# One block in place of nine for the branches of a second model's layer, with the sparse attention's values projected feature-major and turned on TensorE

## The reference

```python
def second_block(x, ...):
    for l in range(DEPTH):
        h = rmsnorm(x, attn_norm_w[l])
        proj = h @ w_in[l]
        (z, xbc, dt_raw, sc_b, sc_c, sc_h, q, k_c, v_c, k_s, v_s, k_w, v_w,
         g_nsa) = jnp.split(proj, split_at, axis=-1)
        y_ssd = ssd_mixer(z, xbc, dt_raw, ...)
        y_sc = sc_b * causal_dwconv(sc_c * sc_h, sc_conv_w[l])
        y_nsa = nsa_mixer(q, k_c, v_c, k_s, v_s, k_w, v_w, g_nsa, ...)
        x = x + jnp.concatenate([y_ssd, y_sc, y_nsa], axis=-1) @ w_out[l]
        h = rmsnorm(x, ffn_norm_w[l])
        ...
```

## Time and profile before

| | us |
|---|---|
| median of 2 runs (4588.11 to 4590.89) | 4589.5 |
| the profiled execution | 4589.26 |
| its span in the profile | 4587.5 |
| layer 0 of the second model, first matmul of its branches to the start of its attention | 2990.1 to 3272.1 |
| the same of layer 1 | 3785.5 to 4067.3 |

### The profile page before, as it was taken

How to read it: one execution, slowest core, us unless ns; L and a number is a source line. 1 busy time by engine, 2 the same in 40 slices (tenths; PEclk the granted TensorE clock), 3 DMA queues, 4 the chain that set the end, 5 groups by cost and what they waited for, 6 DMA issues and landing times. The chain is left out here.

```text
span 4587.5 us, 53132 instructions
## 1 busy us (share of the span) xinstructions
PE 4016.8 (88%) x19582; PEld 3037.8 (66%) x19582; DVE 2268.3 (49%) x3774; ACT 1573.5 (34%) x2671; POOL 299.2 (7%) x292
## 2 busy tenths in 40 slices
PE   4896988998999898878899899886879988678998
PEld 2553566777788795645666688664568877456886
DVE  7777674223653562355532555243455524454552
ACT  2044534112442442245421343233344423333431
POOL 1201010001000000000000100102010010201001
PEclk8997999999999999989999999997899999788999
DMA  6602020111222352000022233220123322012332
GB/s 234 202 8 69 18 96 29 56 61 53 92 96 99 115 165 85 35 17 10 24 69 87 81 98 99 81 75 19 38 64 97 100 98 79 14 33 73 96 98 81
DMA packets 83413, 348.84 MB, mean 76 GB/s; under 512 B 9152, under 2 KB 9536, under 8 KB 79680
## 3 DMA queue, kind: packets, MB, share of 16 engines
q1 hardware_dynamic: 69440, 296.59, 20.0%
q0 software_dynamic: 13824, 50.34, 3.4%
HBM read 344.80 MB, written 2.10 MB: 76 GB/s over the span
## 5 line engine op out<-in xcount | busy, mean ns | idle before, releaser
L556 DVE TENSOR_TENSOR split_low<-weight_ring,split_high 128x1024 fp32r<-128x1024 f32 (+1 forms) x412 | 534.3, 1297 | 818.5 <-ACT split_high L548 818.2
L548 ACT ACTIVATE split_high<-weight_ring 128x1024 fp32r<-128x1024 f32 (+1 forms) x430 | 477.9, 1113 | 969.5 <-PE banks L1197 466.2
L1325 PE MATMUL banks<-normed_high,split_high 128*128 128x512 f32 (+1 forms) x1760 | 652.5, 371 | 79.1 <-DVE normed_low L440 37.9
L1325 PE MATMUL banks<-normed_low,split_high 128*128 128x512 f32 (+1 forms) x1760 | 650.1, 369 | 0.0
L1325 PE MATMUL banks<-normed_high,split_low 128*128 128x512 f32 (+1 forms) x1760 | 649.7, 369 | 0.0
L1325 PEld LDWEIGHTS banks<-normed_high,split_high 128*128 128x128 f32 x1760 | 333.9, 190 | 139.9 <-issue 84.4
L1325 PEld LDWEIGHTS banks<-normed_low,split_high 128*128 128x128 f32 x1760 | 334.1, 190 | 55.4
L1325 PEld LDWEIGHTS banks<-normed_high,split_low 128*128 128x128 f32 x1760 | 333.7, 190 | 55.1
L1197 PE MATMUL banks<-hidden_high,split_high 128*128 128x512 f32 (+1 forms) x880 | 325.0, 369 | 7.2 <-DVE split_low L556 7.2
L1197 PE MATMUL banks<-hidden_low,split_high 128*128 128x512 f32 (+1 forms) x880 | 324.5, 369 | 0.0
L1197 PE MATMUL banks<-hidden_high,split_low 128*128 128x512 f32 (+1 forms) x880 | 324.4, 369 | 0.0
(11 more groups left out here) (235 smaller groups left out, 6550.7 us busy)
## 6 DMA issues: line engine op xcount, KB each, us to landing
weight_ring<-in_up SPq DMA_DIRECT2D x220, 512.0 KB, 3.5
weight_ring<-in_down SPq DMA_DIRECT2D x80, 704.0 KB, 4.0
modulation_ring<-in_ada POOLq DMA_DIRECT2D x96, 512.0 KB, 4.5
weight_ring<-in_merge SPq DMA_DIRECT2D x48, 768.0 KB, 4.2
weight_ring<-in_out SPq DMA_DIRECT2D x32, 512.0 KB, 3.5
weight_ring<-in_diff SPq DMA_DIRECT2D x12, 1024.0 KB, 5.5
weight_ring<-in_xbc SPq DMA_DIRECT2D x16, 512.0 KB, 3.7
weight_ring<-in_window SPq DMA_DIRECT2D x6, 1024.0 KB, 4.8
```

What stands on the lines that cost most here:

```text
L548: act.activation(k.splits[0][:, (n0 + panel) % RING, 0:width], k.slot(n0 + panel)[:, 0:width], ACT.Copy).then_inc(k.high_ready.sem, 1)
L556: dve.tensor_tensor(k.splits[1][:, s, 0:width], k.ring[:, s, 0:width], k.splits[0][:, s, 0:width].bitcast(F32), ALU.subtract).then_inc(k.l ...
L1325: last = pe.matmul(sums(r, half), w, x, start=(c + j == 0), stop=(c == KT - 1 and j == 2))
```

## The change

Blocks 1 to 9 become one block (the norm at its start is kept). Every engine has one hand-written order:

- The four narrow jobs for dt and the gates become one full job with features on the partitions (`steps2`, dt in rows 0 to 7 and gates in rows 32 to 43, the rest zeros), first of all; a few transposes turn the result. The four narrow jobs for the values become one full job (job 24), whose tile four transposes turn (`turn_values`), with a copy by ACT. There are 25 full jobs now: 0 steps, 1 to 8 convolved, 9 to 12 z, 13 to 18 short convolution, 19 to 23 keys and queries, 24 values.
- Results rotate through three PSUM banks; the other five serve the branches' own products.
- Between two jobs TensorE takes a piece of the branches' work: the steps' transposes behind job 5, x's behind job 9, C B^T behind jobs 10 and 11, one head around each of jobs 13 to 20 (spread, job, four weighings), the swaps of rope, the compression and the norm's sums behind jobs 21 to 24.
- DVE's and ACT's operations of steps, short convolution, rope, gather, norm and compression stand between the splits of the panels.
- The compression's weights no longer pass through the ring; four DMAs on SP's queue bring 2 MB into tiles that the state space has left.
- The ring of split panels is 1024 wide here instead of 1408, and the branches have 40 tiles instead of 35.

The diff, cut to its core:

```diff
-    with k.nc.Block() as block:
-        normalise(block)
-        project_split(k, [tile_job(m, tile[:, 24 + m, :]) for m in range(6)], 6, lambda panel: KT * P, block)
-    short_convolution(k, [tile[:, 24 + m, :] for m in range(2)], [tile[:, 26 + m, :] for m in range(2)],
-                      [tile[:, 28 + m, :] for m in range(2)],
-                      k.vec(f"sc_conv{l}").rearrange("p (a b) -> p a b", a=3), [mixed[:, 4 + m, :] for m in range(2)])
...
-    jobs += [token_job(12, t, 20, token_major[:, t, :]) for t in range(4)]
-    project_split(k, jobs, 13, lambda panel: KT * (P if panel < 12 else 20))
...
-    step_sizes(k, l, token_major, gates, rows, columns)
-    state_space(k, l, tile[:, 12:16, :], tile[:, 8:10, :], tile[:, 10:12, :], tile[:, 16:20, :],
...
-    jobs += [token_job(5, t, P, values[:, t, :]) for t in range(4)]
-    project_split(k, jobs, 6, lambda panel: KT * P)
...
-    rope(k, [(q[:, 0, :], "64"), (q[:, 1, :], "64"), (both, "64", 64), (ks, "64"), (kw, "64")])
...
-    compress(k, l, both, gathered, hid_rows, hid, cmp_keys, cmp_values)
...
+CONVOLVED = 8
+GATED = range(1 + CONVOLVED, 5 + CONVOLVED)
+HEADS = 8
+WITH_HEADS = 5 + CONVOLVED
+LAST_JOB = WITH_HEADS + 11
...
+    def bank(q):
+        return k.psum[:, q % 3, 0:LAT]
+    def stored(q):
+        return k.product_stored(1 if q == 0 else q + 1 - CONVOLVED)
+    def turned(r):
+        return stored(WITH_HEADS + 6 + r)
...
+        @block.sync
+        def _(sp):
+            for panel in range(LAST_JOB + 1):
+                sp.wait_ge(*k.low_ready(panel + 1))
+                k.load_panel(sp, n0 + panel + RING)
+                if panel == WITH_HEADS + HEADS:
+                    sp.wait_ge(*k.output_ready(4 * HEADS))
+                    for part in range(4):
+                        sp.dma_start(cmp_weights[:, part, :], k.inp[f"cmp2_{l}"][part]).then_inc(
+                            k.blocks_landed.sem, 16)
...
+            def job(q):
+                pe.wait_ge(*k.low_ready(q + 1))
+                if q >= 3:
+                    if 1 <= q - 3 <= CONVOLVED:
+                        pe.wait_ge(*k.taps_added(3 * (q - 3)))
+                    else:
+                        pe.wait_ge(*stored(q - 3))
+                for c in range(KT):
+                    if q == 0:
+                        pe.wait_ge(*k.normed_ready(c + 1 - KT))
+                    for i, (w, u) in enumerate(triple(split_parts(k, n0, q, c * P),
+                                                      (highs[:, c, :], lows[:, c, :]))):
+                        last = pe.matmul(bank(q), w, u, start=(c + i == 0), stop=(c == KT - 1 and i == 2))
+                last.then_inc(k.product_ready.sem, 1)
...
+            def spread_total(h):
+                if h >= 2:
+                    pe.wait_ge(*k.decay_argument(4 * (h - 1)))
+                else:
+                    pe.wait_ge(*k.turned_copied(8))
+                pe.matmul(select_bank(h), k.table("select")[0:8, h * P:(h + 1) * P], total, start=True,
+                          stop=True).then_inc(k.scores_ready.sem, 1)
+            def weigh_head(h):
+                rows = slice(64 * (h % 2), 64 * (h % 2) + 64)
+                if h >= 4 and h % 2 == 0:
+                    pe.wait_ge(*k.output_stored(h - 3))
+                for j in range(4):
+                    n = 4 * h + j
+                    pe.wait_ge(*k.weights_ready(n + 1))
+                    pe.matmul(pair_bank(h // 2)[rows, j * P:LAT], xdt[:, j, 64 * h:64 * h + 64],
+                              k.probs[:, n % 4, j * P:LAT], start=(j == 0), stop=(j == 3)).then_inc(
+                                  k.output_ready.sem, 1)
...
+            def swap(r):
+                pe.wait_ge(*turned(r))
+                if r >= 1:
+                    pe.wait_ge(*k.sine_part(r))
+                pe.matmul(k.psum[:, 7, 0:LAT], k.table("swap_64"), turns[r][0], start=True, stop=True).then_inc(
+                    k.rope_swapped.sem, 1)
...
+            def turn_values():
+                pe.wait_ge(*stored(LAST_JOB))
+                for t in range(4):
+                    last = pe.transpose(k.psum[:, 4, t * P:(t + 1) * P], mixed[:, 7, t * P:(t + 1) * P],
+                                        k.table("ident"))
+                last.then_inc(k.steps_turned.sem, 1)
...
+            job(0)
+            for m in range(CONVOLVED):
+                job(1 + m)
+                if m == 4:
+                    turn_steps()
+            job(9)
+            turn_x()
+            job(10)
+            products_of_group(0)
+            job(11)
+            products_of_group(1)
+            job(12)
+            for h in range(HEADS):
+                spread_total(h)
+                job(WITH_HEADS + h)
+                weigh_head(h)
+            job(21)
+            swap(0)
+            swap(1)
+            job(22)
+            swap(2)
+            multiply_blocks()
+            job(23)
+            swap(3)
+            turn_blocks()
+            sum_squares()
+            job(LAST_JOB)
+            swap(4)
+            pe.wait_ge(*k.block_gated(2))
+            pe.matmul(k.psum[:, 5, 0:B], w2[:, 0:P], hid[:, 0:B], start=True, stop=True)
+            pe.matmul(k.psum[0:B, 3, 0:64], hid[:, 32:32 + B], w2[:, P:P + 64], start=True, stop=True).then_inc(
+                k.block_product.sem, 1)
+            turn_values()
...
+            def next_high(q):
+                if q < LAST_JOB:
+                    split_high(k, act, n0, q + 1, KT * P, k.product_ready(q) if q else None)
...
+            for h in range(HEADS):
+                next_high(WITH_HEADS + h)
+                for j in range(4):
+                    n = 4 * h + j
+                    act.wait_ge(*k.decay_argument(n + 1))
+                    view = k.probs[:, n % 4, j * P:LAT]
+                    act.activation(view, view, ACT.Exp).then_inc(k.decay_ready.sem, 1)
+                store(WITH_HEADS + h, scale=64 ** -0.5 if WITH_HEADS + h == 20 else 1.0)
+            next_high(21)
+            store(21, scale=64 ** -0.5)
+            next_high(22)
+            store(22)
+            next_high(23)
+            act.wait_ge(*k.block_product(1))
+            act.activation(hid_rows, k.psum[0:64, 3, 0:P], ACT.Gelu_apprx_tanh).then_inc(k.block_gated.sem, 1)
+            for c in range(4):
+                act.wait_ge(*k.output_stored(2 * c + 2))
+                act.activation(k.probs[:, c, 0:LAT], mixed[:, c, :], ACT.Square).then_inc(k.squares_ready.sem, 1)
+            store(23)
+            act.wait_ge(*k.block_product(2))
+            act.activation(hid, k.psum[:, 4, 0:64], ACT.Copy).then_inc(k.block_gated.sem, 1)
+            act.wait_ge(*k.squares_summed(1))
+            act.activation(k.probs[:, 0, 0:LAT], k.psum[:, 6, 0:LAT], ACT.Sqrt, bias=k.scalars[:, 12:13],
+                           scale=1.0 / 512).then_inc(k.deviation_ready.sem, 1)
+            store(LAST_JOB)
+            act.wait_ge(*k.block_product(3))
+            act.activation(cmp_keys, k.psum[:, 5, 0:B], ACT.Copy)
+            act.activation(cmp_values, k.psum[0:B, 3, 0:64], ACT.Copy)
+            act.wait_ge(*k.steps_turned(2))
+            act.activation(tile[:, 33, :], k.psum[:, 4, :], ACT.Copy)
...
+            def next_low(q):
+                if q < LAST_JOB:
+                    split_low(k, dve, n0, q + 1, KT * P, k.high_ready(q + 2))
...
+            next_low(1)
+            taps(0)
+            dve.wait_ge(*k.steps_argument(2))
+            dve.tensor_scalar(r1, r2, 1.0, None, ALU.add).then_inc(k.steps_value.sem, 1)
+            dve.wait_ge(*k.steps_value(2))
+            link(dve.tensor_scalar(r3, r1, -1.0, None, ALU.add))
+            link(dve.tensor_scalar(r5, r3, 1e-30, None, ALU.max))
+            link(dve.reciprocal(r5, r5))
+            next_low(2)
+            taps(1)
...
+            for h in range(HEADS):
+                dve.wait_ge(*k.scores_ready(h + 1))
+                for j in range(4):
+                    n = 4 * h + j
+                    if n >= 4:
+                        dve.wait_ge(*k.output_ready(n - 3))
+                    dve.tensor_scalar(k.probs[:, n % 4, j * P:LAT], select_bank(h)[:, j * P:LAT],
+                                      columns[:, 16 * j + 8 + h:16 * j + 9 + h], 0.0, ALU.subtract,
+                                      ALU.min).then_inc(k.decay_argument.sem, 1)
+                next_low(WITH_HEADS + h)
+                if h >= 2 and h % 2 == 0:
+                    finish_pair(h // 2 - 1)
+                if h >= 6:
+                    convolve(h - 6)
+            next_low(21)
+            finish_pair(3)
+            rotate(0)
+            gather()
+            rotate(1)
+            next_low(22)
+            rotate(2)
+            next_low(23)
+            rotate(3)
+            dve.wait_ge(*k.deviation_ready(1))
+            dve.reciprocal(k.probs[:, 1, 0:LAT], k.probs[:, 0, 0:LAT]).then_inc(k.inverse_ready.sem, 1)
+            rotate(4)
+            dve.wait_ge(*k.inverse_ready(1))
```

(11 more changed lines are left out.)

612 lines of the change are left out of this document (267 added, 345 removed).

## The result

The changed kernel takes 4433.3 us, the median of two runs (4430.6 to 4436.1), against 4589.5 before: a ratio of 0.966, with an interval of 0.962 to 0.970. It is faster by 3.4%. The profiled execution is the one of 4430.6 us; its span is 4428.8.

The account below looks back on a forecast made before the run. Seams between blocks were taken to leave TensorE idle 62 of 282.0 us per layer; the terms 138.6 + 6.8 + 7.5 + 28.3 + 17.5 + 4.6 + 6 gave 209.3, so 4589.3 - 145.4 = 4444 us, range 4424 to 4482.

Parts of the forecast that it names:

- some 15: Sign of being right: TensorE idle some 15 us between the branches' first matmul and the attention's first.
- jobs (one at half clock, 24 at 5.44): 25 full jobs per layer: the first 8.0 us at half clock, the other 24 at 5.44, 138.6 us.
- pauses at jobs 3, 4, 5 and 8: Early jobs: TensorE waits for DVE's splits behind step-size work, 3.6, 1.7 and 0.5 us, then DVE catches up.
- 16 transposes, 8 products: State space's small work on TensorE: 7.5 us per layer, bounds 6.5 and 8.4.
- eight heads beside their jobs: State-space heads: 3.54 us of TensorE each, 28.3 for eight; with its job a head takes 9.0 us.
- behind the heads, and the tail: Swaps, compression and sum of squares with a transpose 17.5 us, then the tail with the attention's start 4.6.
- clock: Half-clock loss behind two pauses, step sizes and compression: 3 us each, 6 per layer, bounds 0 and 16.
- costs nothing: ACT's share of the step sizes is hidden, since a job hides 3.4 us of ACT; otherwise 7.0 us.
- the reserve: In each head, POOL's last weight comes 0.4 us early, plus about 2 more since TensorE asks for it last.
- contention: Rival: DVE and POOL hinder each other in the heads, up to 2 us a head, 4476 us; 14 in 100.
- The clock did not stay low: Rival: jobs and small products run at half clock through the heads, 54 us a layer, 4552 us; 5 in 100.
- Anything outside the two stretches that changed by more than 2 us: Sign of being wrong: a change over 2 us outside the rewritten branch stretches of the second model's two layers.

Follow-up runs that it names:

- the last kernel: Changed kernel with splits ahead of the step sizes, scaling before the last key's turn, and next high half always ahead of the Silu: 4415.6 us, ratio 0.9605.
- the spread-behind-the-job kernel: Changed kernel with each head's spread product behind its job instead of ahead of it: 4526.0 us, ratio 0.986.
- the kernels with more POOL work: Changed kernel with two or four useless 128x256 POOL multiplications added per head: 4443.0 us (0.968) with two, 4474.5 us (0.974) with four.
- the scaling-first kernel: Changed kernel with DVE scaling the four normed tiles before turning the last key: 4430.4 us, ratio 0.965.
- the last two: Changed kernel with splits first and scaling first together, 4426.0 us; and the same with the pause left at job 6 also removed, 4415.6 us.
- measured again: The changed kernel, unaltered, run once more as reference beside the first three experiments: 4436.1 us, ratio 0.966.

## Why the prediction was right, point by point

The forecast was 4444 us, the result is 4433.3, inside the range of 4424 to 4482 and faster as expected. Of the 11 us, 9.6 are in the two stretches (155.0 measured for 145.4); in the profiled runs the first model gives 7.7 more and the attentions take 4.1 back. TensorE was idle 10.3 us in the stretch of layer 0, not the "some 15" that were named as a sign.

Laid out along layer 0, each term beside what the trace has:

| term | predicted | measured |
|---|---|---|
| jobs (one at half clock, 24 at 5.44) | 138.6 | 138.6 |
| pauses at jobs 3, 4, 5 and 8 | 3.6 + 1.7 + 0.5 + 0 | 3.64 + 0 + 1.00 + 1.28 |
| turns of the step sizes | 1.0 | 1.25 |
| 16 transposes, 8 products | 7.5 | 6.4 |
| eight heads beside their jobs | 28.3 | 28.5 |
| behind the heads, and the tail | 22.1 | 21.8 |
| clock | 6 | 1.8 |
| sum | 209.3 | 204.3 |

**The jobs.** From 2982.34 to the first pause, which begins at 3001.22, are 18.88 us: 8.0 + 2 x 5.44 to the hundredth. The jobs' own cost held everywhere that no pause was near.

**The pauses.** The first was worked out from DVE's queue at 3.6, and it is 3.64. The second, 1.7 at job 4, did not appear, for a reason that the prediction kept in another term: behind the first pause job 3 ran partly at half clock and took 6.93 us (3004.86 to 3011.79), and meanwhile DVE had job 4's low half ready, at 3011.73. The clock's loss and this pause are the same time, and the sum had them both. The third, predicted 0.5, is 1.00. The fourth, at job 8, was not predicted at all, and it is ACT's. That ACT's share of the step sizes "costs nothing" was a step that failed: it cost 1.28 us a layer. The total, 5.9 us for 5.8, agrees by luck: one pause too many and one too few. The 3.4 us of room in a job held on average, but the gates' Sigmoid and the Silu behind it each need a table load of 1.28 us, and both stand ahead of the high half of that job. ACT's timeline:

```profile
3030.74 0.78 ACT L1724 ACTIVATE branch_tiles<-banks,small_vectors 128x512 f32<-128x512 f32 x1 [4.14 <-PE banks L1576]
...
3031.71 1.28 ACT L1740 ACT_TABLE_LOAD   x1
3033.00 0.21 ACT L1740 ACTIVATE branch_tiles<-banks 128x48 f32<-128x48 f32 x1
3033.23 1.28 ACT L1702 ACT_TABLE_LOAD   x1
...
3035.06 1.05 ACT L557 ACTIVATE split_high<-weight_ring 128x1024 fp32r<-128x1024 f32 x1
```

and DVE's, which waits for it:

```profile
3036.14 1.23 DVE L565 TENSOR_TENSOR split_low<-weight_ring,split_high 128x1024 fp32r<-128x1024 f32 x1 [2.27 <-ACT split_high L557]
```

The centre tap could not start before job 6 ended (3030.6), and from there ACT has 5.4 us of queue in front of a job that is needed 5.4 us later, with DVE's 1.2 still to come. The room of a job must be counted from the wait it starts behind, not as idle time. With the high half ahead of them, as in the last kernel, the loads cost nothing. The Trainium skill (ScalarE: Activation LUTs, What ACT_TABLE_LOAD costs) adds to each load of about 1.28 us another 1.38 for draining; the load's 1.28 agrees, and the drain is not here: the Sigmoid starts 1.29 us after its load does, and 0.02 us lie between the operation ahead of the first load and the load.

**The heads** came at 9.01 us for 9.0. The reasoning that a job hides the head's chain held: the spread-behind-the-job kernel is the counter-proof (15.3 us a head in layer 0, 13.9 in layer 1), and the kernels with more POOL work measure the reserve. The reserve was put at 0.4 for the last weight and about 2 more, without contention; 1.3 are left with the contention's 1.15 in it, so the 2.4 were right and half of them are used.

**Behind the heads** the second swap waits 0.87 (predicted 0.75), the 64 products of the compression take 7.4 us, not 8.3 (they now follow each other without a pause between panels; the 8.3 was four times a panel by itself), the squares 3.1, not 3.6. Nothing waits for the compression's four transfers. The tail is 4.64 us for 4.6, with TensorE idle 3.52 of it ("about 5" was named as a sign); the scaling-first kernel shows that 2.2 of it was DVE's order.

**The clock** was the mis-sized term: 6 taken, 1.8 measured. It makes 8.4 of the 9.6 us. Inside the block only the 3.64 us pause has a price in clock. The two jobs behind it, 48 matmuls, take 12.7 us in place of 10.9 (3004.86 to 3017.57); in TensorE's timeline the first seven of them start 0.42 to 0.59 us apart, the rest mostly 0.23. Behind the pauses of 1.00 and 1.28 us the very next matmuls stand 0.33 and then 0.23 apart, full clock. The prediction charged 3 us each to the step sizes and to the compression, and the compression has no pause long enough: 0.98 granted. One such pause at the 2.5 us of the earlier trace rows would have given 205.8.

**The transposes and products** were taken from a stretch that ran partly at half clock; between jobs they run at the full one, 16 transposes in 1.7 us and eight products in two lots of 2.1, with 0.6 us in the seams with the jobs.

TensorE's timeline around them:

```profile
3048.44 1.91 PE L1593 MATMUL banks<-ones_and_identity,branch_tiles 128*128 128x128 f32 x16
3050.10 0.48 PE L1576 MATMUL banks<-normed_high,split_high 128*128 128x512 f32 x1
...
3055.64 2.32 PE L1602 MATMUL banks<-branch_tiles 128*128 128x512 f32 x8
```

**The other rivals.** The clock did not stay low, and no pause for a bank's store appeared. "Anything outside the two stretches that changed by more than 2 us" was named as a sign against: the attentions with their feed-forwards grew by 2.2 and 1.9. TensorE's busy time there is 1.8 us larger with the same matmuls in layer 0 (471.04 against 469.26), so it is clock: the first row is the kernel before, the second the kernel after, five microseconds from the start of the attention, of which the earlier kernel has 0.78 granted and the later 0.50.

```profile
3272.10:3277.10 5.00, 2.58 (x15) 1.56 (x15) 2.98 (x22) 3.26 (x11) 0.00 (x0) 0.78 0.11 43
```

```profile
3186.60:3191.60 5.00, 3.17 (x15) 1.98 (x15) 2.97 (x22) 3.27 (x11) 0.00 (x0) 0.50 0.01 2
```

Before, TensorE's last pause ahead of the attention was 0.62 us; now it is 3.52. With 1.31 us there the first five microseconds have 0.58 granted in the scaling-first kernel and 0.73 and 0.70 in the last two, yet the attention stretches of layer 0 are 514.39, 515.90 and 516.09 us long: the shortest goes with the lowest of the three. So the shorter wait gave 1.2 us back in one kernel and nothing in two, and what sets the length of this stretch is open.

The medians' difference, 156.2 us (and 156.6 when measured again), is 5 us more than the 151.0 that the two stretches and the attentions explain. All twelve profiles together do not show that the first model is faster in the changed kernels; whether these 5 us are scatter is open.

## What to carry to other kernels

When blocks are fused so that one engine never stops, write out each helper's queue from the moment it is released to the moment its result is asked for, with table loads in it. The averages (2 of 5.44 us busy) hid the one pause that nobody foresaw. Put what the bounding engine asks for next at the head of each helper's queue, ahead of anything that itself waits: that order, the tail's 2.2 us included, was worth 10 us a layer here, more than the change of the product's shape. And price a pause by its length: here pauses of 1.0 and 1.3 us between dense jobs cost their own length, 3.6 cost 5.4, and 2.85 in every head nearly double.
